# Hybrid decoder trunk on one core: projection pieces of S5 and retention put at other places in passes 0 and 2

## The reference

```
h = rmsnorm(x, norm_w[l])                         # width 1024
proj = h @ w_in[l]                                # 1024 x 3592, cut into the inputs below
s5_out = s5_mixer(s5_x, ...)                      # diagonal complex state space, 16 groups x 64
hg_out = head_norm(gated recurrence of hg_q, hg_f, hg_i)
ml_out = head_norm(sigmoid(ml_o) * mlstm(ml_q, ml_k, ml_v, ml_i, ml_f))
rt_out = head_norm(retention(rotary(rt_q), rotary(rt_k), rt_v))
mixed = concat(s5_out*silu(s5_g), hg_out*silu(hg_g), ml_out*silu(ml_g), rt_out*silu(rt_g))
x = x + mixed @ w_out[l]
```

## Time and profile before

| what | us |
|---|---|
| median of 3 runs | 1565.33 |
| lowest and highest | 1562.23, 1573.06 |
| the profiled execution, its own time | 1563.95 |
| its span in the profile | 1562.1 |
| TensorE busy | 1375.1 (88%) |
| VectorE, ScalarE, GpSimd busy | 887.8, 551.8, 450.3 |

### The profile page before, as it was taken

One profiled execution on the slowest core, in us unless ns is written; L12 is line 12 of the kernel. 1 busy time (PEld: TensorE's weight loads), 2 busy tenths in 40 slices (PEclk: granted clock), 3 DMA queues, 4 the chain that ended last, 5 costly groups with the idle time before them and its releaser, 6 DMA issues.

```text
span 1562.1 us, 31689 instructions
## 1 busy us (share of the span) xinstructions
PE 1375.1 (88%) x12391; PEld 1206.8 (77%) x12391; DVE 887.8 (57%) x2670; ACT 551.8 (35%) x1197; POOL 450.3 (29%) x628
## 2 busy tenths in 40 slices
PE   2868899989887898998999899998999899789886
PEld 2757788778776888886778789878878799779665
DVE  4986746464795516455655536646465444644546
ACT  4435443343323523322443234334433423321011
POOL 4342434431002433231310254443100533331001
PEclk9989899989998999998999999998999899999988
DMA  6222123431234332372313332343123314456501
GB/s 175 95 81 70 55 83 109 145 105 62 75 108 121 102 77 87 85 108 69 112 63 116 109 100 83 110 144 115 60 68 110 99 57 123 136 87 115 148 9 59
DMA packets 167563, 149.84 MB, mean 96 GB/s; under 512 B 63440, under 2 KB 155352, under 8 KB 165752
## 3 DMA queue, kind: packets, MB, share of 16 engines
q1 hardware_dynamic: 96696, 76.38, 18.3%
q10 hardware_dynamic: 70720, 71.44, 15.8%
HBM read 124.42 MB, written 23.37 MB: 95 GB/s over the span
## 4 chain that ended last, share of the span: by engine, by line
PE 61%; DVE 16%; ACT 6%; DMA 5%; issue 5%; POOL 4%; SPq 2%; DVEq 0%; ACTq 0%; POOLq 0%
PE psum L2347 17%; PE psum L2352 16%; PE psum L2681 5%; DVE r L1686 4%; PE psum L2659 3%; PE psum L2600 3%; DVE r L2060 3%; DMA wraw<-in_w_in 2%; POOL wlo L1152 2%; PE psum L2599 1%; ACT r L1467 1%; PE psum L2511 1%; PE psum L2419 1%; POOL rs L1177 1%; PE psum L2597 1%
## 5 line engine op out<-in xcount | busy, mean ns | idle before, releaser
L1152 POOL TENSOR_TENSOR wlo<-wraw,whi 128x256 fp32r<-128x256 f32 (+1 forms) x448 | 350.9, 819 | 414.2 <-ACT whi L1196 408.7
L2352 PE MATMUL psum<-whi,hhi 128*128 128x256 f32 (+1 forms) x896 | 272.2, 304 | 14.0 <-ACT th L1283 12.2
L2352 PE MATMUL psum<-whi,hlo 128*128 128x256 f32 (+1 forms) x896 | 262.9, 293 | 0.0
L2352 PE MATMUL psum<-wlo,hhi 128*128 128x256 f32 (+1 forms) x896 | 262.8, 293 | 0.0
L2347 PE MATMUL psum<-hhi,whi 128*128 128x288 f32 (+2 forms) x672 | 231.9, 345 | 7.0 <-ACT r L1317 4.8
L2347 PE MATMUL psum<-hhi,wlo 128*128 128x288 f32 (+2 forms) x672 | 220.5, 328 | 0.0
L2347 PE MATMUL psum<-hlo,whi 128*128 128x288 f32 (+2 forms) x672 | 220.3, 328 | 0.0
L2352 PEld LDWEIGHTS psum<-whi,hhi 128*128 128x128 f32 x896 | 181.1, 202 | 22.9 <-issue 14.9
L2352 PEld LDWEIGHTS psum<-wlo,hhi 128*128 128x128 f32 x896 | 181.1, 202 | 0.7 <-issue 0.5
L1174 POOL TENSOR_SCALAR rs<-mv 128x4 f32<-128x4 f32 (+1 forms) x54 | 10.4, 192 | 594.0 <-DVE mv L2243 591.3
L2352 PEld LDWEIGHTS psum<-whi,hlo 128*128 128x128 f32 x896 | 180.4, 201 | 0.0
(11 more groups left out here) (355 smaller groups left out, 2319.8 us busy)
## 6 DMA issues: line engine op xcount, KB each, us to landing
wraw<-in_w_in ACTq DMA_DIRECT2D x50, 1024.0 KB, 5.4
wraw<-in_w_out ACTq DMA_DIRECT2D x14, 1024.0 KB, 5.4
x<-xo SPq DMA_DIRECT2D x48, 128.0 KB, 2.3
r<-x SPq DMA_DIRECT2D x10, 512.0 KB, 5.3
r<-in_c_rot SPq DMA_DIRECT2D x4, 1088.0 KB, 7.5
wraw<-in_w_in ACTq DMA_DIRECT2D x4, 1056.0 KB, 6.2
r<-WTm SPq DMA_DIRECT2D x4, 1024.0 KB, 13.7
r<-VTm SPq DMA_DIRECT2D x4, 1024.0 KB, 6.3
```

The costliest lines, as they stand in the source:

```text
L1152: nc.gpsimd.tensor_tensor(wlo[:, hslot[b], ks, 0:width], wraw[:, wslot[b], ks, 0:width], whi[:, hslot[b], ks, 0:width].bitcast(F32), ALU.s ...
L2352: mm = nc.tensor.matmul(bank.t[:, 0:width], x[:, kt, c], w[:, sl, kt, 0:width], start=first, stop=last)
```

## The change

In passes 0 and 2 the order is now: `rt_qk`, `rt_v` and `s5_g` beside mLSTM; then the four halves of `s5_x` with their `take` and `u`, with no mixer step between; then the first piece of `rt_g`, `prenorm` 0 and `prenorm` 1; then retention woven with the other pieces of `rt_g`, `prenorm` 2 and 3, and `norm` 0 to 4. The old branch stays for pass 1. Pass 3 is as it was. The whole diff:

```diff
--- before.py
+++ after.py
@@ -152,12 +152,12 @@
 
     passes = range(2 * DEPTH)
 
-    def project(n, br, after=None):
+    def project(n, br, after=None, only=None):
 
 
         out, late = [], []
         for b in BLOCKS:
-            if b[0][:2] == br and br in parts:
+            if b[0][:2] == br and br in parts and b[0] in (only or BLOCK):
                 ks = pieces_of_block(n, b[0])
                 for k in ks:
                     out += [(("proj", n, b[0]), ("mm", k))] + late
@@ -271,9 +271,25 @@
         for t in range(NCH) if n + 1 not in passes and beside else ():
             k = beside.index((("proj", n, "rt_v"), ("mm", (n, "rt_v", t))))
             beside.insert(k + 1, (("final",), t))
-        plan += weave(mix(n, "ml"), beside)
+        if n % 2 == 0 and "rt" in parts and "s5" in parts:
+            beside = project(n, "rt", only=("rt_qk", "rt_v")) + project(n, "s5", only=("s5_g",))
+            plan += weave(mix(n, "ml"), beside) + project(n, "s5", {"s5_x": s5(n, "u")}, only=("s5_x",))
+            gates = project(n, "rt", only=("rt_g",))
+            tiles = norm(n + 1)
+            k = tiles.index((("norm", n + 1), 1))
+            tiles = [(("prenorm", n + 1), 2), (("prenorm", n + 1), 3)] + tiles
+            rows = [(("prenorm", n + 1), 0), (("prenorm", n + 1), 1)]
+            plan += gates[:1] + rows + weave(mix(n, "rt"), gates[1:] + tiles)
+        else:
+            plan += weave(mix(n, "ml"), beside)
         half = project(n, "s5", {"s5_x": s5(n, "u")})
-        if n + 1 in passes:
+        if n + 1 in passes and n % 2 == 0 and "rt" in parts and "s5" in parts:
+            plan += s5_beside(n)
+            head = mix(n + 1, "hg")
+            filler, rest = outs(n), s5set(1) if n == 0 else []
+            if rest:
+                filler = spread(filler[:13], rest[:8]) + filler[13:14] + rest[8:10] + filler[14:15] + rest[10:12] + filler[15:] + rest[12:]
+        elif n + 1 in passes:
             plan += weave(mix(n, "rt"), with_rows(half, n + 1) + norm(n + 1))
             plan += s5_beside(n)
```

## The result

The changed kernel takes 1600.49 us (median of 4, 1597.03 to 1606.59) beside 1563.78 for the one before: a ratio of 1.021, 95% interval 1.017 to 1.025. Forecast were 1593, between 1572 and 1605, and slower by over 1% with a chance of 0.79. A second set of four executions gave 1599.46 and 1.020 (1.016 to 1.024).

A forecast was written before the change was run, and what follows sets the result against it. TensorE, busy 88% of the span, was taken as the bound. New idle time gave +9.9 us a pass, half clock made it +14.9, or +29.8 in two passes on 1563.95: 1593.8, stated as 1593, range 1572 to 1605.

The forecast's parts named there:

- The first gap: TensorE's wait before retention chunk 0's `C` in passes 0 and 2, mask behind GpSimd's split: 6.0 us idle.
- The second gap: TensorE's wait before retention chunk 1's `D`, whose `N` stands behind prenorm 2 and 3: 5.4 us idle.
- The tail: Retention chunk 2's `C` to S5's `w`: idle 2.1, 1.1, 0.9 and 2.8 us, `w` at 47.3.
- The clock: Half clock after the two new TensorE waits: 3.3 and 1.75 us, bringing +9.9 to +14.9 us a pass.
- the old wait before mLSTM's `D`: TensorE's 2.85 us wait before mLSTM chunk 3's transpose, said to stay unchanged, with five dense 3.05 us halves behind.
- its sign: Pass 2's 3.04 us idle before mLSTM's `D`, followed by a gate piece of 4.59 us instead of 3.08.
- The base: Profiled execution's own 1563.95 us, to which 29.8 was added for 1593.8; 1.4 more if counted from the median.
- (a): Rival: faster, as norm tiles are spread and the crowding before `w` goes: 8.2 us a pass, 1547.5; chance 0.06.
- (b): Rival: no change, chunk 0 stalls but VectorE does prenorm 2 and 3 beside it: 1565 to 1572; chance 0.14.
- (c): Rival: slower still, long half clock after each gap: 20.2 us a pass, 1604; chance 0.12 for 1600 and above.
- my own case: The forecast itself, both waits with some half clock after them: 1580 to 1600 us, chance 0.68.
- the price of three retention chunks without projections: Last retention chunks lose projections as cover; they replace the old crowding's 5.4 us idle, within +9.9 us a pass.

The follow-up runs named there:

- e1: Changed kernel with prenorm 0 and 1 moved from ahead of retention B0 0 to behind N 0: 1575.67 us, ratio 1.0071.
- e4: Changed kernel with, on GpSimd alone, the split of hg_f behind the powers of prenorm 0 and 1: 1577.82 us, ratio 1.0082.
- e6: Kernel before with the first s5_x half, its weight split, then prenorm 0 and 1 ahead of retention B0 0: 1587.98 us, ratio 1.0144.
- e7: Kernel before with prenorm 0 and 1 alone ahead of retention B0 0, ahead of the weight split too: 1570.53 us, ratio 1.003.
- e2: Changed kernel with prenorm 2 and 3 moved ahead of retention's gate piece 3: 1592.34 us, ratio 1.0167.
- e8: Changed kernel with prenorm 0 to 3 beside the s5_x halves and prenorm 4 behind N of chunk 2: 1568.36 us, ratio 1.000.
- e10: Changed kernel with prenorm 0 to 3 beside s5_x, prenorm 4 behind chunk 2's N, mLSTM chunk 3's D behind the last s5_g half: 1562.94 us, 0.9965.
- e9: Kernel before with prenorm 4 behind chunk 3's N and mLSTM chunk 3's D behind retention's last gate piece: 1552.60 us, ratio 0.991.

## Why the prediction was right

**The first gap.** Forecast: mask 13.1 us after the last `s5_x` half, idle 6.0. Measured: `C` 0 at 306.13, 13.1 after 293.05, idle 6.41. All its links held: the split 5.56 (5.59 taken), the second power 1.46 beside a scaling, the first 0.56 with none beside it. The Trainium skill, GPSIMD Engine Reference, section 1, names the interface that GpSimd shares with VectorE; the trace agrees in this pair of rows. e1 shows that the wait is that of the rows ahead of the mask; e4 (4.0 of 6.4 us) and e6 beside e7 (5.6 us) show that the split ahead of the powers is the larger part of it.

**The second gap.** Forecast 5.4 before `D` 1, measured 5.73. `D` 1 stands 35.0 us after the last `s5_x` half; forecast were 31.6 at full clock and 3.3 for the clock before it. That clock came as taken: half for 6.5 us after the first gap, against 6.8 in the sum:

```profile
306.13:312.60 6.47, 6.47 (x36) 6.18 (x37) 2.69 (x16) 0.00 (x0) 1.25 (x2) 0.50 0.09 29
```

The mechanism held, but e2 gives back only 8.2 us, as the queue behind it has its own delays.

**The tail.** `C` 2 at 38.1 (34.9 and 3.3 forecast), `w` at 52.8 (47.3 and 5.05). Waits of 0.75 before `C` 2 and 2.25 before `D` 3, forecast 2.1 and 2.8, and none of the 1.1 before `D` 2 and 0.9 before `C` 3: TensorE's steps took longer at half clock and filled that time (norm tile 2 took 1.97 us at 335.13, where 1.09 is full clock). Half clock behind the second gap was longer than the sum had it, 0.67 over 17.78 us, that is 11.7 us at half:

```profile
328.04:345.82 17.78, 14.78 (x90) 12.49 (x90) 13.22 (x46) 4.93 (x11) 2.84 (x5) 0.67 0.00 1
```

It cost no more than the 1.75 taken, since here VectorE's chain sets the pace, as the prediction says.

**The clock.** +14.9 us a pass forecast, 17.1 and 15.3 measured in the two stretches. What I had left out is half clock after the old wait before mLSTM's `D`: it was 3.10 us here, and the five half pieces after it took 16.75 us in pass 0 and 15.73 in pass 2, where at full clock they take 14.2. My sum had 15.25 for them, five times 3.05, about 1 too much for full clock; this hid a part of what was missing. The term mis-sized is thus the cost of a wait that the edit doesn't touch. The prediction had its sign before it and read past it: it says that pass 2 repeats pass 0 within 0.2 us, which holds for the last window of the earlier trace rows but not for the whole stretch, 60.38 against 58.84, and nearly all of the difference is the gate piece of 4.59 us after that wait. The Trainium skill, TensorE: Matmul & The Clock Gate, Part 1, says that the place of the transition varies from run to run, and the executions of e1 agree with those of the changed kernel: the same steps and the same 3.10 us were followed by 14.2 us in one and by 16.75 in the other. So no single execution prices it.

**The base.** My 1593 missed the 1600.5 by 7.5 us: 2.6 are the two stretches (32.4 for 29.8). The rest, 4.9, is not tied to any place. In the second set's profiled execution (1598.62) the stretches to `w` are 32.3 longer than before and everything outside them 2.4. The medians of before alone went from 1563.8 to 1567.9 in four sets. That the number came within half a percent is thus partly luck. One smaller reading was wrong without effect: the DMAs that move with `u` did not go some 25 us earlier (the loads of `U` begin at 300.63, before at 301.19).

**The rivals.** (a) fell with the first gap. (b) fell with the second: VectorE did not keep up. (c), the long half clock, has its price in part: 17.1 and 15.3 of its 20.2. By number, 1600.49 lies just at the 1600 from which (c) was counted and outside the 1580 to 1600 of my own case, the second set's 1599.46 just inside; by mechanism the first gap was followed by 6.5 us of half clock, as in the forecast, and not by the 13.6 of (c). What the prediction called the price of three retention chunks without projections is small beside the 32 us of the rows, but it is there: e8 has these chunks and is at 1.000, and e10 stays 10.3 us behind e9.

## What to carry to other kernels

A step moved in a list that all engines share is moved in every queue: follow the smallest product of the slowest queue (here a power of one column on GpSimd) and look what stands ahead of it. A long wait that costs nothing, like VectorE's 7.54 us on `rstd`, is a warning: what is placed behind it waits too, and TensorE pays what its own work doesn't cover (6.41 us here). Rows of preparation can go where their engine idles (e8), and a transpose that waits for a head norm belongs behind one more piece (e9). Compare two orders only after each has had such repairs: e8 alone seemed to say that the place of the pieces is free, and e9 beside e10 says otherwise.

## What the runs showed that was not expected

e1 gave back 13 us of waits in the profiled execution and 24.8 in the median. Its stretches, 23.4 us shorter, account for nearly all of it: the waits, the half clock that followed them, and 2.5 us of half clock that came or stayed away by itself. e4 is the one that stays unexplained: 10.3 us in the stretches, 22.7 in the median. Part of that lies outside the stretches, where the order is the same, and part in the spread of its executions; how the order of one stage moves half-clock stretches in later ones stayed open, and no run here was made to tell that apart.
